# Four pairs of experts, written out one by one, each with one class number and one chain of tests

## The reference

```python
def _moe_swiglu(x, w_r, b_r, w_up, w_down):
    logits = (x @ w_r + b_r).astype(jnp.float32)
    top_v, top_i = lax.top_k(logits, TOP_K)
    gates = jax.nn.softmax(top_v, axis=-1)
    gate_e = jnp.sum(jax.nn.one_hot(top_i, N_EXPERTS, dtype=jnp.float32) * gates[..., None], axis=-2).astype(x.dtype)
    y = jnp.zeros_like(x)
    for e in range(N_EXPERTS):
        y = y + gate_e[..., e:e + 1] * _swiglu(x, w_up[e], w_down[e])
    return y
```

## Time and profile before

| what | value |
|---|---|
| median of three runs | 2446.11 us (2443.81 to 2448.54) |
| the profiled execution | 2438.56 us, span 2436.1 us |
| mean granted TensorE clock | 0.953 of full speed |
| PE busy | 2210.7 us, 91% |
| DVE, ACT, POOL busy | 473.6, 397.8, 88.3 us |
| DMA, mean | 200 GB/s |

### The profile page before, as it was taken

One profiled execution on the slowest core, in us unless ns is written; L12 is line 12 of the kernel. 1 busy time (PEld: TensorE's weight loads), 2 busy tenths in 40 slices (PEclk: granted clock), 3 DMA queues, 4 the chain that ended last, 5 costly groups with the idle time before them and its releaser, 6 DMA issues.

```text
span 2436.1 us, 35753 instructions
## 1 busy us (share of the span) xinstructions
PE 2210.7 (91%) x14427; PEld 1594.2 (65%) x14428; DVE 473.6 (19%) x1119; ACT 397.8 (16%) x820; POOL 88.3 (4%) x165
## 2 busy tenths in 40 slices
PE   8997878898999989888788869999799989899996
PEld 5764548766776757645687659964799458737743
DVE  2333215332000024231254230000100010000002
ACT  2114422202000021245221120000100000000002
POOL 0000310000000000013000000000000000000000
PEclk9999889899999999999798979999899999989998
DMA  9536883131333233379501038787387749996991
GB/s 307 154 120 248 305 310 98 40 121 57 125 125 112 85 104 121 106 270 321 193 1 40 35 122 293 278 293 259 133 300 257 299 159 386 393 363 249 353 395 61
DMA packets 217556, 486.47 MB, mean 200 GB/s; under 512 B 15072, under 2 KB 94636, under 8 KB 211218
## 3 DMA queue, kind: packets, MB, share of 16 engines
q1 hardware_dynamic: 203570, 437.10, 50.5%
q0 software_dynamic: 13792, 46.74, 5.7%
HBM read 474.81 MB, written 8.98 MB: 199 GB/s over the span
## 4 chain that ended last, share of the span: by engine, by line
PE 74%; DVE 8%; DMA 5%; ACT 4%; issue 4%; SPq 2%; POOL 0%; DVEq 0%; POOLq 0%; ACTq 0%
PE ps L750 19%; PE ps L829 17%; PE ps L896 9%; PE ps L793 4%; PE ps L866 3%; PE ps L1119 2%; PE ps L809 2%; PE ps L916 2%; PE ps L1036 2%; DMA ring<-in_moe_w_down_dram 2%; DMA ring<-in_moe_w_up_dram 1%; PE ps L734 1%; PE ps L940 1%; PE ps L744 1%; PE ps L725 1%
## 5 line engine op out<-in xcount | busy, mean ns | idle before, releaser
L829 PE MATMUL ps<-region,ring 128*128 128x224 f32 (+1 forms) x2816 | 435.8, 315 | 6.0 <-DMA ring<-in_moe_w_up_dram 6.0
L829 PEld LDWEIGHTS ps<-region,ring 128*128 128x128 f32 x2816 | 423.7, 191 | 26.3 <-issue 24.5
L750 PE MATMUL ps<-hT,ring 128*128 128x320 f32 x1472 | 398.4, 434 | 5.3 <-ACT hT L1461 5.3
L750 PEld LDWEIGHTS ps<-hT,ring 128*128 128x128 f32 x1472 | 280.3, 191 | 122.5 <-ACT hT L1461 5.9
L896 PE MATMUL ps<-ring,big 128*128 128x512 f32 (+1 forms) x528 | 233.0, 597 | 7.4 <-DMA ring<-in_moe_w_down_dram 7.4
L896 PEld LDWEIGHTS ps<-ring,big 128*128 128x128 f32 (+1 forms) x528 | 93.6, 181 | 138.5 <-issue 125.9
L2220 DVE TENSOR_TENSOR big<-hT,ps 128x896 f32<-128x896 f32 (+3 forms) x24 | 19.9, 827 | 476.2 <-PE ps L829 476.2
L744 PE MATMUL ps<-mean,onesm 128*128 128x128 f32 x738 | 102.8, 293 | 4.0 <-ACT ctmp L1542 1.7
L744 PEld LDWEIGHTS ps<-mean,onesm 128*128 128x128 f32 x738 | 95.3, 205 | 11.4 <-issue 4.1
L793 PE MATMUL ps<-big,ring 128*128 128x320 f32 x352 | 95.3, 433 | 1.0 <-DVE big L2194 1.0
L866 PE MATMUL ps<-ring,region 128*32 128x256 f32 (+2 forms) x960 | 86.8, 418 | 0.0
(11 more groups left out here) (346 smaller groups left out, 2112.2 us busy)
## 6 DMA issues: line engine op xcount, KB each, us to landing
ring<-in_moe_w_up_dram SPq DMA_DIRECT2D x144, 1024.0 KB, 8.1
ring<-in_moe_w_down_dram SPq DMA_DIRECT2D x80, 1024.0 KB, 9.9
ring<-in_ada_w_dram SPq DMA_DIRECT2D x48, 1024.0 KB, 6.8
region<-in_cache_v_dram SPq DMA_DIRECT2D x128, 256.0 KB, 5.2
ring<-in_w_in_dram SPq DMA_DIRECT2D x28, 1024.0 KB, 5.4
ring<-in_moe_w_up_dram SPq DMA_DIRECT2D x32, 768.0 KB, 5.7
ring<-in_dense_w_up_dram SPq DMA_DIRECT2D x22, 1024.0 KB, 5.1
region<-in_cache_k_dram POOLq DMA_DIRECT2D x64, 256.0 KB, 3.9
```

Source lines behind the costliest of these rows:

```text
L750: m = mm(ps[:, b + o, 0:n], w[:, k, o * P:(o + 1) * P], rhs[:, k, 0:n], start=(first and k == 0), stop=(last and k == nk - 1))
L829: m = mm(ps[:, 2 * part + t // 2, 256 * (t % 2):256 * (t % 2) + n], w[:, kk, t * P:(t + 1) * P], XE[:, k, t0:t0 + n], start=(k == 0 and t ...
```

## The change

Each of the four pairs has code of its own on PE, ACT and DVE: the engine's loop becomes a loop of Python, and the pair's number a constant. DVE computes one class number per pair: the small class plus 3 times the place of the big class in a list, which is (1, 0, 2) for pairs 0 and 1, and (0, 1) for pairs 2 and 3. An engine reads that number once and runs through one chain of tests, one leaf after another, with 8 leaves for the first two pairs and 6 for the others; the last has no test. The zeros in `mixT` are written by POOL when the output projection of layer 1 is done; DVE waits for them. SP's loop stays.

```diff
-        def by_class(eng, c, code):
-            with eng.If(c < 1):
-                code(0)
-            with eng.Else():
-                with eng.If(c < 2):
-                    code(1)
+        def by_code(eng, i, code):
+
+            c = eng.value_load(cls[0:1, i:i + 1], min_val=0, max_val=8)
+            big = (1, 0, 2) if i < 2 else (0, 1)
+            leaves = [(3 * x + cj + 1, ci, cj) for x, ci in enumerate(big) for cj in range(3 if ci < 2 else 2)]
+
+            def chain(k):
+                limit, ci, cj = leaves[k]
+                if k == len(leaves) - 1:
+                    code(ci, cj)
+                    return
+                with eng.If(c < limit):
+                    code(ci, cj)
                 with eng.Else():
-                    code(2)
-
-        def by_pair(eng, cb, cs, code):
-            by_class(eng, cb, lambda ci: by_class(eng, cs, lambda cj: code(ci, min(cj, 1) if ci == 2 else cj)))
-
-        def classes(eng, i):
-            return [eng.value_load(cls[0:1, bass.ds(i + PAIRS * x, 1)], min_val=0, max_val=2) for x in range(2)]
+                    chain(k + 1)
+
+            chain(0)
...
+            pool.wait_ge(s_chunk, POS_WO[1] + 4)
+            nc.gpsimd.memset(mixT[:], 0.0).then_inc(s_fa, KT)
             pool.wait_ge(s_y, 3)
...
-                    with pe.Fori(0, PAIRS) as i:
-                        by_pair(pe, *classes(pe, i), lambda ci, cj: experts(ci, cj, i))
+                    for i in range(PAIRS):
+                        by_code(pe, i, lambda ci, cj: experts(ci, cj, i))
...
-                    with act.Fori(0, PAIRS) as i:
-                        by_pair(act, *classes(act, i), lambda ci, cj: experts(ci, cj, i))
+                    for i in range(PAIRS):
+                        by_code(act, i, lambda ci, cj: experts(ci, cj, i))
...
-                    by_pair(dve, *classes(dve, i), lambda ci, cj: select(ci, cj, eb, es, Sel, 0).then_inc(s_prep, 1))
+                    by_code(dve, i, lambda ci, cj: select(ci, cj, eb, es, Sel, 0).then_inc(s_prep, 1))
...
-                    by_pair(dve, *classes(dve, i), lambda ci, cj: experts(ci, cj, i, eb, es))
+                    by_code(dve, i, lambda ci, cj: experts(ci, cj, i, eb, es))
...
-                    for g, (lo, hi) in enumerate(((BIG_N[0], BIG_N[1]), (SMALL[0][0], SMALL[1][0]))):
-                        V.tensor_scalar(small[:, 32 + 4 * g:36 + 4 * g], small[:, 24 + 4 * g:28 + 4 * g], float(lo), None, ALU.is_gt)
-                        m = V.tensor_scalar(small[:, 40 + 4 * g:44 + 4 * g], small[:, 24 + 4 * g:28 + 4 * g], float(hi), None, ALU.is_gt)
-                    link(m)
-                    V.tensor_tensor(cls[:], small[:, 32:40], small[:, 40:48], ALU.add).then_inc(s_route, 1)
+                    over = lambda o, c0, n, lim, w, op: V.tensor_scalar(small[:, o + c0:o + c0 + n], small[:, 24 + c0:24 + c0 + n],
+                                                                        float(lim), float(w), op, ALU.mult)
+                    over(32, 0, 2, BIG_N[0], 3, ALU.is_le)
+                    over(40, 0, 2, BIG_N[1], 6, ALU.is_gt)
+                    over(32, 2, 2, BIG_N[0], 3, ALU.is_gt)
+                    over(40, 2, 2, BIG_N[1], 0, ALU.is_gt)
+                    over(32, 4, 4, SMALL[0][0], 1, ALU.is_gt)
+                    link(over(40, 4, 4, SMALL[1][0], 1, ALU.is_gt))
+                    link(V.tensor_tensor(small[:, 48:56], small[:, 32:40], small[:, 40:48], ALU.add))
+                    V.tensor_tensor(cls[:, 0:PAIRS], small[:, 48:52], small[:, 52:56], ALU.add).then_inc(s_route, 1)
...
-                    V.memset(mixT[:], 0.0).then_inc(s_fa, KT)
...
+                    dve.wait_ge(s_fa, KT)
                     dve.wait_ge(s_route, 2)
                     prepare_pair(0)
                     link(V.memset(SelG, 0.0))
-                    with dve.Fori(0, PAIRS - 1) as i:
-                        pair(i)
-                    pair(PAIRS - 1, True)
+                    for i in range(PAIRS):
+                        pair(i, i == PAIRS - 1)
```

## The result

Median 2412.74 us (2400.3 to 2419.57, 4 runs) against 2445.67 us (2443.81 to 2448.54, 4 runs) for the kernel before: ratio 0.9861, 95% interval 0.9823 to 0.9899. A second series on one chip gave 2414.08 against 2443.82 us, ratio 0.9881 (0.9859 to 0.9903). The profiled execution was the fastest of the first series, 2400.3 us with a span of 2398.7 us.

A forecast was written before the change was run, and what follows sets the result against it. PE's gaps ahead of the pairs were put down to sequencer jumps, the bodies to PE or, in pair 2, DMA. Gaps 22.4, clock +1.5, POOL -0.3 make 23.6, say 24 us: 2446.1 - 24 = 2422 us, range 2411 to 2435.

The forecast's parts named there:

- pair 0: gap: PE idle ahead of pair 0's pack: its jump goes, DVE's selection table is late next; 5.1 us saved.
- pair 1: gap: PE idle between pairs 0 and 1: only the jump out, a class load and a true test remain; 9.85 us saved.
- pair 1: pack at full clock: Pack of pair 1: half of its 2.9 us half-clock loss comes back, 1.4 us saved.
- pair 2: gap: PE idle between pairs 1 and 2: the jump out of the leaf stays; 6.3 us saved.
- pair 2: pack: Pack of pair 2: half of its 1.8 us half-clock loss comes back, 0.9 us saved.
- pair 3: gap: PE idle between pairs 2 and 3: one jump over the first leaf, taken as 4.3 us; 1.2 us saved.
- zeros on POOL: POOL's memset of mixT beside DVE's residual after the output projection: hindrance taken as 0.3 us lost, up to 3.
- rival 1: New code behind the join: fall-through stalls like a jump, pairs 1 and 2 lose about 4.2 us each; 2431 us, chance 0.17.
- rival 2: Combine of pair 2: its half-clock tail goes too, 4 us more saved; 2418 us, chance 0.2.
- rival 3: Pair 2, bound by DMA: loads don't move with its start, its gap's 7.2 us are lost; 2429 us, chance 0.07.
- rival 4: Tails of the other three pairs: half-clock stretches, about 10 us each, make the kernel slower; 2452 us, chance 0.04.
- rival 5: Jump out of a leaf grows by the back-edge's time; only pair 0's 5.1 - 0.8 us remain; 2442 us, chance 0.03.

The follow-up runs named there:

- e2: Changed kernel, unrolled, but with the two class numbers and nested tests of before: median 2428.08 us, ratio 0.9926 to the kernel before.
- e1: Changed kernel with the zeros of mixT written by DVE again: median 2410.47 us, ratio 0.9857 to the kernel before.
- e3: Kernel before with only the zeros of mixT moved to POOL: median 2443.16 us, ratio 0.9995 to the kernel before.
- e5: Changed kernel with SP's loop unrolled and half of the next pair's first loads held back: median 2412.07 us, ratio 0.9849 to the kernel before.
- c1: The changed kernel run again with nothing different: median 2414.08 us, ratio 0.9881 to the kernel before.

## Why the prediction was right

By its own steps, with the changed kernel's first profile:

| term | forecast | measured |
|---|---|---|
| pair 0: gap | 5.1 | 15.18 - 9.89 = 5.3 |
| pair 0: colder pack | -0.8 | 12.17 - 13.17 = -1.0 |
| pair 1: gap | 9.85 | 12.31 - 2.24 = 10.1 |
| pair 1: pack at full clock | 1.4 | 13.24 - 10.60 = 2.6 |
| pair 2: gap | 6.3 | 8.70 - 2.26 = 6.4 |
| pair 2: pack | 0.9 | 8.35 - 8.35 = 0 |
| pair 3: gap | 1.2 | 1.8 |
| zeros on POOL | -0.3 | 0 |
| stage | 24 | 26.4 |

The measured terms make 25.2 us. The other 1.2 us are about what pair 3 gives, 203.7 us from its pack on in place of 205.0, 1.0 us of it in the pack (9.59 in place of 10.57); the bodies of pairs 0 to 2 differ by 0.5 us or less.

- **The jumps.** What goes, what stays and what each costs came as read from the trace: the jump out at 6.25 us, one read, one true test, gap 2.24 us against 2.4 forecast. e2 shows that it is the jumps, and not the loop as such. *Each leaf still waits for its code* (rival 1) is refuted: the fall-through into code never run took 83 ns.
- **Pair 0.** What was late next was the DVE table, as forecast; the saving was 0.2 us more than forecast. The zeros mattered only there (e1, e3).
- **Pair 3.** The new jump cost 4352 ns where I took 4.3 us, and by the row of 231 ns it would have cost nothing. It hid behind the slow combine. In the loop e3 had 231 ns again, the unrolled kernels 3782 to 4674 ns. The jump of 231 ns fetched nothing (see e5), so its code was at hand; that it was so because pair 2 had just run the leaf beside it fits this, but wasn't tried by itself.
- **The clock.** The two terms of 1.4 and 0.9 us were taken halfway between none and all, and that their sum came near (2.6 and 0) is luck. At pair 1 it wasn't luck of this profile: all nine with a gap of 2.3 us or less there have the pack at full speed (10.5 to 10.6 us). At pair 2 it was: three of the ten unrolled profiles have the slow pack (8.35 to 8.43 us), seven the fast one (6.68 to 6.76 us). *The slow tail goes too* (rival 2) is what e1 and c1 had: pair 2's part 9.5 and 8.2 us shorter (from the start of its pack to the end of its combine, 188.7 and 190.0 us in place of 198.2), of which the exposed jump takes 5.4 and 5.6 us back. I forecast 4 us net; e1's stage, with 1.4 us for its zeros taken off, is 4.9 us shorter, c1's 1.6 us, since the packs of pairs 2 and 3 stayed partly at half clock in c1.
- *Saved time comes back as waiting for weights* (rival 3): pair 2 with a gap of 2.3 us is as long as with 8.7 (198.2 against 197.6 us from the start of its pack to the end of its combine). Refuted.
- *Slower by more half-clock tails* (rival 4) and *no change* (rival 5) didn't occur in any of the runs; the jump out over seven leaves takes 6.25 us against 6.41 before.
- **The total.** The median fell by 33 us in the first series and 30 in the second, the stage by 26 to 28 us in the profiles. I forecast 24. The intervals reach from 25 to 43 and from 24 to 34 us, so the stage alone can explain them; that something ahead of the stage helps by a few us can't be excluded and isn't shown. The median of 2412.74 us is 9 us under the 2422 forecast and 1.7 us above the lower end of the range, 2411. The range had counted 2 us for the scatter of the runs; the four executions of the changed kernel lie 19 us apart. So that the median fell inside the range owes something to luck, while the stage came as its terms say.
- One detail was wrong and harmless: ACT's table load ahead of the pack of pair 1 isn't delayed but gone. The leaves have one table load on ACT in the changed kernel's profile, in place of eight; why wasn't looked into.

## What to carry to other kernels

Put the leaf that runs where the test falls through, and count jumps, not tests: each taken jump to new code is microseconds of an engine's sequencer, a true test is 0.08 us. A jump is free if it ends before the work queued ahead of it does; keep big loads out of the moment in which it fetches its code (5.2 us of the stage here, in one pair of profiles). Compare stage by stage when totals scatter as much as the effect.

## What the runs showed of the hardware

- The same jump out of a leaf took 6.2 us when the DMA share in its first 5 us was 0.94, and 3.5 to 3.7 us at 0.02. One 16 KB packet of the instruction queue moves in it; it started 3.7 us behind the jump's start in the first case and about 1 us in the second. A jump of 231 ns had no such packet.
- A test that is true, with its leaf behind it in line, took 83 ns in front of code that had never run.
- A memset of 2560 columns on POOL (2.23 us) didn't delay a DVE operation with two SBUF inputs beside it: 0.29 us with and without.
- Products that nobody reads, 6.96 us of them in an idle time of 9.8 us, kept the granted clock at its upper level (1.00 in place of 0.50) and made the pack behind it 2.5 us shorter.
- Ahead of the stage, with the same code but for one memset on POOL, the time at half clock differed by 41 us between executions (133 to 174 us), and the start of the stage by 20 us.
